# A Trainium2 kernel for two transformer-like blocks: the first mixer's head sums in column tiles, their factors spread by transfers

## The reference

```python
def _rms_f32(xf):
    return xf * lax.rsqrt(jnp.mean(xf * xf, axis=-1, keepdims=True) + EPS)

def _l2norm(xf):
    return xf * lax.rsqrt(jnp.sum(xf * xf, axis=-1, keepdims=True) + EPS)
...
    q = _l2norm(q.reshape(bsz, s, h, d)) * (d ** -0.5)
    k = _l2norm(k.reshape(bsz, s, h, d))
...
    o = _rms_f32(_from_chunks(o))          # retention
```

## Time and profile before

| | |
|---|---|
| median of 3 runs | 1787.51 us |
| lowest and highest | 1785.11, 1788.03 us |
| profiled execution | 1785.32 us, its span 1783.5 us |
| TensorE busy | 1756.9 us (99%) |
| VectorE busy | 1154.7 us (65%) |
| ScalarE busy | 724.6 us (41%) |
| granted TensorE clock, mean | 0.997 of full speed |

### The profile page before, as it was taken

The page is one execution under the profiler, slowest core; times in us unless marked ns, Lnnn a source line. Parts: engine busy times, 40 slices in busy tenths (PEclk is TensorE's granted clock), DMA queues, the critical chain, the costliest instruction groups (busy, mean ns, idle before and its releaser), DMA issues.

```text
span 1783.5 us, 22826 instructions
## 1 busy us (share of the span) xinstructions
PE 1756.9 (99%) x9228; PEld 1403.4 (79%) x9228; DVE 1154.7 (65%) x1685; ACT 724.6 (41%) x1028; POOL 0.2 (0%) x4
## 2 busy tenths in 40 slices
PE   8999989999999999999999999999998999999999
PEld 6877867888888888766888888888764888888887
DVE  5876954777777344777777777433997667777521
ACT  4257424544443333345644444323224544444311
POOL 0000000000000000000000000000000000000000
PEclk9999999999999999999999999999999999999999
DMA  6222101332222323311322332232662222222232
GB/s 231 92 96 70 55 28 42 129 102 95 95 95 89 99 97 115 104 45 48 124 95 95 101 101 92 96 95 96 188 174 86 95 94 95 95 100 98 87 98 79
DMA packets 57681, 174.35 MB, mean 98 GB/s; under 512 B 8028, under 2 KB 8540, under 8 KB 57448
## 3 DMA queue, kind: packets, MB, share of 16 engines
q1 hardware_dynamic: 57576, 172.89, 29.8%
HBM read 162.07 MB, written 2.12 MB: 92 GB/s over the span
## 4 chain that ended last, share of the span: by engine, by line
PE 96%; DVE 2%; ACT 1%; issue 1%; DMA 0%; SPq 0%; DVEq 0%; ACTq 0%
PE bank L201 95%; DVE mixer_arena L1188 1%; PE bank L617 0%; DMA raw<-in_w_in 0%; DVE mixer_arena L1196 0%; DVE res L1188 0%; DVE even_arena L1716 0%; ACT even_arena L749 0%; DVE wl L1188 0%; ACT wh L749 0%; DVE mixer_arena L1481 0%; DVE mixer_arena L1192 0%; DVE gdn_low_ygl L1188 0%; SPq L1892 0%; PE bank L393 0%
## 5 line engine op out<-in xcount | busy, mean ns | idle before, releaser
L201 PE MATMUL bank<-nh,wh 128*128 128x512 f32 x1520 | 602.9, 397 | 8.3 <-DVE nl L1196 8.2
L749 ACT ACTIVATE wh<-raw 128x1024 fp32r<-128x1024 f32 (+2 forms) x310 | 308.8, 998 | 707.7 <-PE bank L201 696.5
L201 PE MATMUL bank<-nl,wh 128*128 128x512 f32 x1520 | 593.2, 390 | 0.0
L201 PE MATMUL bank<-nh,wl 128*128 128x512 f32 x1520 | 593.0, 390 | 0.0
L1188 DVE TENSOR_TENSOR wl<-raw,wh 128x1024 fp32r<-128x1024 f32 (+2 forms) x310 | 355.4, 1147 | 245.2 <-ACT wh L749 244.4
L201 PEld LDWEIGHTS bank<-nh,wh 128*128 128x128 f32 x1520 | 286.2, 188 | 76.9 <-DVE wl L1188 9.0
L201 PEld LDWEIGHTS bank<-nl,wh 128*128 128x128 f32 x1520 | 286.4, 188 | 62.0 <-issue 3.4
L201 PEld LDWEIGHTS bank<-nh,wl 128*128 128x128 f32 x1520 | 286.2, 188 | 60.3
L201 PE MATMUL bank<-ff_yh,wh 128*128 128x512 f32 x528 | 205.4, 389 | 0.0
L201 PE MATMUL bank<-ff_yl,wh 128*128 128x512 f32 x528 | 205.4, 389 | 0.0
L201 PE MATMUL bank<-ff_yh,wl 128*128 128x512 f32 x528 | 205.4, 389 | 0.0
(11 more groups left out here) (182 smaller groups left out, 1413.0 us busy)
## 6 DMA issues: line engine op xcount, KB each, us to landing
raw<-in_ff_a_up SPq DMA_DIRECT2D x44, 512.0 KB, 3.4
raw<-in_ff_b_up SPq DMA_DIRECT2D x44, 512.0 KB, 3.4
raw<-in_ff_c_up SPq DMA_DIRECT2D x44, 512.0 KB, 3.4
raw<-in_w_in SPq DMA_DIRECT2D x32, 512.0 KB, 3.5
raw<-in_pw SPq DMA_DIRECT2D x24, 512.0 KB, 3.7
raw<-in_even_in SPq DMA_DIRECT2D x16, 512.0 KB, 3.4
conf_shifted<-conf_pad SPq DMA_DIRECT2D x112, 66.0 KB, 2.1
raw<-in_ff_a_down_a SPq DMA_DIRECT2D x8, 512.0 KB, 3.5
```

Source lines behind the costliest of these rows:

```text
L201: return e.matmul(out, lhsT, rhs, start=start, stop=stop, skip_group_check=True)
L749: return e.activation(out, in_, func, **kw).then_inc(n.give(sem), 1)
```

## The change

Four heads share one bank. Each head's squares are multiplied by 32 columns of ones only, and the result goes to 32 of the bank's partitions, so that one bank holds the four sums of a group, each 32 times. There are three groups (keys, retention outputs, queries) and three sum banks. ScalarE takes one Ln and one Exp for a group, into `m1.hroot[g]`. SyncE then copies each head's 32 rows four times, to the four quarters of the partitions of `m1.hsq[i]`: 16 transfers for a group, ahead of the raw loads of pieces 30, 31 and 32. VectorE waits for a group's transfers before the group's first scaling; the scaling itself stays. The keys' root is taken before the queries' squares instead of behind them. The retention scale 1/P and the keys' and queries' scale 1 stay as they were. To make room for three semaphores, the forget rows of the attention stage share two semaphores instead of having four.

```diff
-    def head_sum(i):
-
-        e.wait_ge(c.head_squared, i + 1)
-        if i >= 6:
-            e.wait_ge(c.head_logged, i - 5)
-        mm(bank[m1.sum_bank[i % 6]][:, :], c.ones[:, :], m1.hsq[i], True, True).then_inc(n.give(c.head_summed), 1)
+    def head_sums(g):
+
+        e.wait_ge(c.head_squared, HEADS * (g + 1))
+        for h in range(HEADS):
+            done = mm(bank[m1.sum_bank[g]][h * Q:(h + 1) * Q, :], c.ones[:, 0:Q], m1.hsq[HEADS * g + h], True, True)
+        done.then_inc(n.give(c.head_summed), 1)
...
         if i == 9:
             e.wait_ge(c.gcols_ready, 1)
-            for q in range(4):
-                head_sum(q)
+            head_sums(0)
         if i == 10:
             e.wait_ge(c.ret_copied, HEADS)
-            for q in range(4, 6):
-                head_sum(q)
+            head_sums(1)
         if i == 11:
-            for q in range(6, 12):
-                head_sum(q)
+            head_sums(2)
...
             if t == 0:
-                e.wait_ge(c.head_logged, 12)
+                e.wait_ge(c.head_logged, 3)
                 e.wait_ge(c.head_scaled, 12)
...
-    def head_root(src, dst, logged, rooted, count, scale):
-
-        for q in range(count):
-            act(dst(q), src(q), ACT.Ln, logged, bias=c.eps[:, 0:1], scale=scale)
-        settle()
-        for q in range(count):
-            act(dst(q), dst(q), ACT.Exp, rooted, scale=-0.5)
...
+    def roots_of(g, scale):
+        e.wait_ge(c.head_summed, g + 1)
+        act(m1.hroot[g], bank[m1.sum_bank[g]][:, :], ACT.Ln, c.head_logged, bias=c.eps[:, 0:1], scale=scale)
+        settle()
+        act(m1.hroot[g], m1.hroot[g], ACT.Exp, c.head_root, scale=-0.5)
...
         if i == 10:
+            roots_of(0, 1.0)
             square_heads(m1.gq, 8)
-            roots_of(0, 4, 1.0)
         if i == 11:
-            roots_of(4, 2, 1.0 / P)
-
-    roots_of(6, 2, 1.0 / P)
-    roots_of(8, 4, 1.0)
+            roots_of(1, 1.0 / P)
+
+    roots_of(2, 1.0)
...
     def head_scale(i):
-        e.wait_ge(c.head_root, i + 1)
+        if i % HEADS == 0:
+            e.wait_ge(c.head_spread[i // HEADS], 16 * HEADS * NB)
...
-        e.wait_ge(c.row_ready[h % 4], 16 * (h // 4 + 1))
+        e.wait_ge(c.row_ready[h // 2 % 2], 32 * (h // 4 + 1))
...
+    def spread_heads(g):
+
+        e.wait_ge(c.head_root, g + 1)
+        for h in range(HEADS):
+            for b in range(NB):
+                load(m1.hsq[HEADS * g + h][b * Q:(b + 1) * Q, :], m1.hroot[g][h * Q:(h + 1) * Q, :], c.head_spread[g])
...
+        if 30 <= s < 33:
+            spread_heads(s - 30)
         if s == 32:
             e.wait_ge(c.head_scaled, 12)
```

More of the change, by code:

```diff
@@ L162, in allocate @@
         bank=[ctx.enter_context(nc.psum_tensor(f"bank{i}", [P, S], F32)) for i in range(8)],
+        head_spread=[ctx.enter_context(nc.semaphore(f"head_spread{i}")) for i in range(3)],
         raw_ready=[ctx.enter_context(nc.semaphore(f"raw_ready{i}")) for i in range(RAWS)],
@@ L165, in allocate @@
         shifted=[ctx.enter_context(nc.semaphore(f"shifted{i}")) for i in range(KEPT)],
-        row_ready=[ctx.enter_context(nc.semaphore(f"row_ready{i}")) for i in range(HEADS)],
+        row_ready=[ctx.enter_context(nc.semaphore(f"row_ready{i}")) for i in range(2)],
         x_ready=[ctx.enter_context(nc.semaphore(f"x_ready{i}")) for i in range(DK)],
@@ L1904, in forget_row @@
     def forget_row(h):
-        load(m2.nrow[:, h % 4, :], d["forget_rows"][h:h + 1, :].broadcast_to([P, S]), c.row_ready[h % 4])
+        load(m2.nrow[:, h % 4, :], d["forget_rows"][h:h + 1, :].broadcast_to([P, S]), c.row_ready[h // 2 % 2])
     def chunk(k):
@@ L2019, in build @@
             rows=slots(A, 22), d=c.sq[:, 0, :].rearrange("p (t s) -> p t s", s=P),
-            hsq=[slots(A, i) for i in (19, 20, 21, 22, 16, 17, 4, 5, 12, 13, 14, 15)], sum_bank=(6, 7, 2, 3, 4, 5),
+            hsq=[slots(A, i) for i in (19, 20, 21, 22, 16, 17, 4, 5, 12, 13, 14, 15)], sum_bank=(6, 7, 2), hroot=[c.sq[:, 0, :], c.sq[:, 1, :], c.acc[:, :]],
             oret=slots(A, 0, 4), kbg=slots(A, 4, 4), kd=slots(A, 8, 4), vb=slots(A, 12, 4), gg=slots(A, 0, 4),
```

## The result

| | before | after |
|---|---|---|
| median of 4 runs each, us | 1786.88 (1785.11 to 1788.03) | 1801.80 (1801.30 to 1802.50) |
| ratio after to before | | 1.0079, 95% interval 1.0067 to 1.0092 |
| profiled execution, time / span, us | 1785.3 / 1783.5 | 1801.3 / 1799.5 |

The change makes the kernel 14.9 us slower. The forecast, 1804.5 us, had the direction and lay 2.7 us too high; the range holds the time. (Two executions further down, 4555 us of the kernel with all spreads first and 2534 us of the kernel before beside it, are far outside all others, and the ratios leave them out.)

What follows compares the result with a forecast made beforehand. TensorE, busy for 99% of the span, was taken to bound the kernel. Late first transposes (14.9 us) plus lower clock (2.1) gave +17.0 on the median 1787.5: 1804.5 us, range 1792 to 1810.

Steps and rivals of the forecast that it cites:

- Sums: TensorE's three groups of head sums: 1.19 us a group, 3.6 in all against 10.5, list shorter by 6.9 us.
- Wait for the squares: TensorE, before the second group of sums: waits 2.3 us for ScalarE's retention squares, ending at 166.88.
- Keys' factor: ScalarE: the keys' Ln and Exp, 0.65 us each, have the factor out at 169.85 us.
- Issue price: SyncE's transfers: 0.633 us an issue as in the conformer's shift, 10.13 us for a group's 16.
- First transposes: TensorE, first chunk: start at 205.65 instead of 190.75, 14.9 us late, after VectorE's scaling of the queries.
- Clock: TensorE after about 20 us of waiting: a lower granted clock adds 2.1 us.
- Merged semaphores: Forget rows: the first addition waits for two rows instead of one, at a cost of 0 us.
- nothing behind it can take it back: Behind the first chunk: the 2.1 us of clock loss stay to the end, as the chain there is TensorE's.
- The step from a profiled execution to the median: Profiled execution 1785.3 us lies 2.2 under the median 1787.5; adding 17.0 to that median gives 1804.5 us.
- the cheap issues (1) and (2): SyncE's transfers: issues at 0.46 us, 1796.1 us, chance 0.16; or hidden transfers at the array's pace, 1785.7 us, chance 0.05.
- the dear case (4): Transfers landing after 5 us among weight loads, clock low for longer: +22 us or more, 1810 and up, chance 0.05.
- the third: Rival on TensorE: column tiles don't run together, sums save nothing; 1802 to 1805 us, counted within the forecast's 0.70.

## Why the prediction came out as it did

Right, step by step, with forecast and measurement (the first block of sums starts 0.65 us earlier in the profiled run of after than in that of before, so its times read 0.65 low):

- **Sums**: forecast 1.19 us a group with the change of form; measured 1.07 us a block. TensorE done with its pieces: forecast 185.8, measured 185.2.
- **Wait for the squares**: forecast 2.3, measured 2.29.
- **Keys' factor**: forecast 169.85, measured 168.95. Queries' factor: 178.1 against 177.3.
- **Issue price**: forecast 10.13 us for 16, measured 10.62, 10.55 and 10.02. End of the third run: forecast 201.5 (its last issue from 200.9), measured 201.5. Landing: 2.1 against 2.0. The nearest row, the conformer's shift, was the right one; the forget-row loads (0.46) and the single load (0.33) were not.
- **First transposes**: forecast 205.65, measured 205.55. Counted from the first sums they are 15.45 us late, against a forecast of 14.9; the two longer runs (0.9 us together, less what was gained at the keys' factor and the loads) make that half microsecond.
- **Clock**: forecast 2.1. Measured between the first transposes (14.80 late) and the next piece's second matmul (210.53 against 193.67, 16.86 late; the row of before stands below): 2.06 us. That this is within 0.1 us is luck in part: 2.1 was picked between 1.4 and 2.5, without a sum that gives it.
- **Merged semaphores**: forecast 0; the delay is the same to 0.1 us before and behind the forget rows.

Timeline of TensorE, kernel before, second matmul behind the first chunk's block:

```profile
193.67 0.39 PE L201 MATMUL bank<-nl,wh 128*128 128x512 f32 x1
```

Wrong in size, by 2.7 us in all. The steps above add up to 17.5 us when counted from the first sums (15.45 + 2.06), half a microsecond more than forecast; that the profiled execution of the kernel after reached the first sums 0.65 us earlier hides this, and leaves 16.86 behind the chunk. The rest: (1) "nothing behind it can take it back" failed: 0.75 us came back in the level stage, where the two low-clock stretches of the kernel before were absent (that they are the cause is read from the rows, no run isolates it); with 0.13 more behind it the span grew by 16.0 instead of 17.0. (2) The step from a profiled execution to the median: I added 17.0 to 1787.5. Against 1786.88, the median with one more run, that is 0.6; and before's profiled execution lay 1.6 under its median, after's only 0.5, which is the remaining 1.1. The sum was better than the base it was put on, with its own two misses in opposite directions.

Of the rivals, the cheap issues (1) and (2) are excluded by the three runs of 16, the dear case (4) by the landing of 2.0 and the clock's 2.06, the third by the blocks of 1.07. The statement that the time "is set by issues" was only a sum until the quarter of the bytes and the second queue showed it. What failed were my expectations afterwards, three of them in one term: for the kernels through DRAM (1787 to 1790, 1783 and 1782 expected; 1792.4, 1790.8 and 1788.7 measured) I priced a store and its load back from the one instance that had the queue to itself. The kernel without the wait for squares (1780 to 1781 expected, 1783.6 measured) missed by the landing of the retention factors: VectorE's scaling starts at 188.02, 4.9 us after the last of their loads was issued (183.09). The two queues missed by 1 to 3 us on GpSimd's wait for its own landing.

## What to carry to other kernels

Count DMA issues, not only bytes: 16 transfers of 32 partitions on one queue took 10 to 11 us with 64 KB as with 16 KB in each, and a chain of short engine work that now passes through them is bound by the queue. Before shortening one engine's list at a crossing, look how late the other engine is: here TensorE and VectorE met within 0.1 us, so neither the shorter sums nor the other order of scalings moved the time alone beyond the spread, and both together did once the factors came in time and TensorE had no squares to wait for. A small store that something waits for belongs ahead of large transfers, or some time behind them (here 1.7 to 1.8 us with nothing issued in the 3 us before it, 3.6 to 5.1 directly behind).

## What the runs showed of the hardware that I had not expected

- An issue on SyncE for a transfer between partitions of SBUF, 32 partitions wide, takes 0.62 to 0.69 us with 64 KB and 0.63 to 0.68 with 16 KB (means of runs of 8 or 16); on GpSimd eight with 64 KB take 3.9 to 4.05 us, 0.49 to 0.51 each.
- A store of four rows to DRAM until the queue goes on: 1.7 to 1.8 us with no other issue in the 3 us before it, 2.2 behind loads issued 1.1 us earlier, 3.6 to 3.8 directly behind four 256 KB loads, 4.6 to 5.1 with a 512 KB load there as well.
- A load that spreads one DRAM row over 128 partitions (256 KB) is one issue of 0.44 us and lands after a median 3.6 us.
- TensorE's rate behind a wait of 2.3 us is not the same from run to run of the same instructions: 1.07 us for the block behind it in the kernel after, 1.67 without the transfers, 1.93 with the filler matmuls. The granted clock from 169 to 171 is 1.00, 0.50 and 0.67 in these. The runs spread widely too, 1780.97 to 1789.89 without the transfers, with a granted clock over the whole of 0.998 in the fastest and 0.992 in the slowest; that waits like this one make all of that spread is not shown. Differences under 2 us between kernels are therefore read from the trace here, not from medians.
